# Modulation rows from unsplit weights in four column groups, and attention outputs taken by pairs of tiles, in a fused diffusion step

## The reference

```python
mod = silu(cond) @ w_ada + b_ada            # cond: 2 rows (latent, context), w_ada 1024 x 6144
shift_a, scale_a, gate_a, shift_f, scale_f, gate_f = split(mod, 6)
h = rmsnorm(x) * (1 + scale_a) + shift_a
q, k, v, g, za_f, za_b, u = split(h @ w_in)
o = gla(q, k, v, decay(za)) ; o = rmsnorm(o) * silu(g)     # 4 heads, both directions, chunks of 64
p = (pooled(u) - u) @ w_pool * pool_scale                  # 4 channel groups
x = x + gate_a * (concat(o, p) @ w_out)
h = rmsnorm(x) * (1 + scale_f) + shift_f
x = x + gate_f * expert_choice_moe(h)                      # 16 SwiGLU experts, 80 tokens each, d_ff 2816
```

## Time and profile before

| | us |
|---|---|
| median of three runs (lowest, highest) | 1903.52 (1901.79, 1906.20) |
| the profiled execution, its own time | 1903.08 |
| span of its profile | 1901.3 |
| PE busy (share of the span) | 1847.0 (97%) |
| DVE busy | 1551.7 (82%) |
| ACT busy | 1250.7 (66%) |

### The profile page before, as it was taken

How to read it: one execution, slowest core, us unless ns; L and a number is a source line. 1 busy time by engine, 2 the same in 40 slices (tenths; PEclk the granted TensorE clock), 3 DMA queues, 4 the chain that set the end, 5 groups by cost and what they waited for, 6 DMA issues and landing times.

```text
span 1901.3 us, 25073 instructions
## 1 busy us (share of the span) xinstructions
PE 1847.0 (97%) x9056; PEld 1500.9 (79%) x9056; DVE 1551.7 (82%) x1254; ACT 1250.7 (66%) x1002; POOL 272.7 (14%) x120
## 2 busy tenths in 40 slices
PE   6998879999999999999999999999999999999998
PEld 2777667668888888888888888888888888888886
DVE  4632854689889898989898989898989898989897
ACT  4433642356767676767676767676767677777774
POOL 1000000010202030303030302030303030303060
PEclk9999989989999999999999999999999999999999
DMA  8522532689999999999999999999999999999993
GB/s 287 178 76 85 184 128 89 221 313 390 389 384 390 384 381 385 368 385 373 386 372 387 372 386 371 383 373 387 375 382 374 385 372 387 372 383 370 393 378 123
DMA packets 280812, 622.83 MB, mean 328 GB/s; under 512 B 12461, under 2 KB 46018, under 8 KB 280778
## 3 DMA queue, kind: packets, MB, share of 16 engines
q1 hardware_dynamic: 273664, 598.68, 85.8%
q0 software_dynamic: 6064, 20.72, 3.7%
q10 hardware_dynamic: 1050, 2.97, 0.4%
HBM read 607.19 MB, written 15.14 MB: 327 GB/s over the span
## 4 chain that ended last, share of the span: by engine, by line
PE 93%; DVE 4%; ACT 1%; issue 1%; DMA 0%; ACTq 0%; DVEq 0%
PE bank L1831 17%; PE bank L1832 17%; PE bank L1835 17%; PE bank L1861 8%; PE bank L1857 8%; PE bank L1856 8%; PE bank L1416 3%; PE bank L1418 3%; PE bank L1417 3%; PE bank L1841 1%; PE bank L1451 1%; PE bank L1661 1%; DVE w_lo L945 1%; PE bank L1468 0%; PE bank L1469 0%
## 5 line engine op out<-in xcount | busy, mean ns | idle before, releaser
L1278 DVE TENSOR_TENSOR w_lo<-raw,w_hi 128x2048 fp32r<-128x2048 f32 x528 | 1197.7, 2288 | 121.7 <-ACT w_hi L845 119.6
L845 ACT CAST w_hi<-raw 128x2048 fp32r<-128x2048 f32 x524 | 997.8, 1913 | 181.2 <-PE bank L1835 104.3
L1831 PE MATMUL bank<-w_hi,xe_hi 128*128 128x512 f32 (+1 forms) x1536 | 573.8, 380 | 0.0
L1832 PE MATMUL bank<-w_hi,xe_lo 128*128 128x512 f32 (+1 forms) x1536 | 563.4, 373 | 0.0
L1835 PE MATMUL bank<-w_lo,xe_hi 128*128 128x512 f32 (+1 forms) x1536 | 380.4, 373 | 0.0
L1831 PEld LDWEIGHTS bank<-w_hi,xe_hi 128*128 128x128 f32 x1536 | 290.0, 189 | 49.6 <-issue 1.7
L1832 PEld LDWEIGHTS bank<-w_hi,xe_lo 128*128 128x128 f32 x1536 | 290.3, 189 | 48.5
L1835 PEld LDWEIGHTS bank<-w_lo,xe_hi 128*128 128x128 f32 x1536 | 273.4, 188 | 51.8
L1857 PE MATMUL bank<-w_hi,hT_lo 128*128 128x512 f32 x700 | 273.0, 390 | 0.0
L1856 PE MATMUL bank<-w_hi,hT_hi 128*128 128x512 f32 x700 | 272.7, 390 | 0.0
L597 POOL DMA_INDIRECT acc_dram<-yrow,idx_s x15 | 43.6, 2910 | 1072.6 <-DVE yrow L1320 1072.6
(11 more groups left out here) (264 smaller groups left out, 1367.6 us busy)
## 6 DMA issues: line engine op xcount, KB each, us to landing
raw<-in_w_e_gate SPq DMA_DIRECT2D x176, 1024.0 KB, 11.0
raw<-in_w_e_up SPq DMA_DIRECT2D x176, 1024.0 KB, 11.3
raw<-in_w_e_down SPq DMA_DIRECT2D x176, 1024.0 KB, 10.9
raw<-in_w_ada SPq DMA_DIRECT2D x16, 1024.0 KB, 5.1
raw<-in_w_in SPq DMA_DIRECT2D x8, 1024.0 KB, 5.6
ada_f<-in_w_ada SPq DMA_DIRECT2D x4, 1024.0 KB, 16.6
raw<-in_w_out SPq DMA_DIRECT2D x4, 1024.0 KB, 5.0
ada_raw<-in_w_ada SPq DMA_DIRECT2D x4, 1024.0 KB, 12.2
```

Of the source, the lines that this page charges most:

```text
L845: nc.scalar.copy(hi_slot(j), raw[:, raw_slot(j), :]).then_inc(hi_done, 1)
L1278: nc.vector.tensor_tensor(lo_slot(j), raw[:, raw_slot(j), :], hi_slot(j), ALU.subtract).then_inc(lo_done, 1)
L1831: nc.tensor.matmul(out, xe_hi[:, kk, :], wh[:, k, :], start=kk == 0, stop=False)
L1832: nc.tensor.matmul(out, xe_lo[:, kk, :], wh[:, k, :], start=False, stop=False)
```

## The change

All modulation blocks take the weights as loaded: `spread` multiplies the four blocks of contracted rows of a unit with the 32-column `cond`, each into its own 32 partitions of the bank, and the second unit (kh = 1) adds onto the first; the four partial sums are added after the turn, by a reduction in `mod_columns`. `ada_turn` turns 128 rows in place of 2 or 4, `mod_rows` copies 128. The casts and rests of the 16 ada units go; their raw slots are released by PE (`ada_used`), and the split slots are counted for the input and output projections alone (`split_count`). The position rows go to four banks without a wait between. Block 9 moves into the last tile of the loop, ahead of the pooling. `gate_a` is spread by DMA, over `gate_dram`, on POOL's queue. The pooled `mix` blocks come ahead of the attention outputs, these are taken as tiles (0, 1), (2, 3) and (4), each with its own squares and norm, and the pooled half of the first output product (tile 0, half 0) goes ahead of the turn of the heads. `gate_rows` runs in column groups too, and all of it before the choice of tokens ends.

```diff
+POS_BANKS = (4, 6, 2, 3)
+WIN_UNITS = 7
+NSPLIT = WIN_UNITS + 4
...
+def split_count(n):
+    return n - WIN0 if n < ADA0 else WIN_UNITS + n - WOUT0 + 1
 def pre_split(n):
-    return n % SPLIT if n < NPRE - 1 else SPLIT
+    if n < ADA0:
+        return (split_count(n) - 1) % SPLIT
+    return n - WOUT0
+def slot_user(n):
+    users = [q for q in range(n) if PRE[q][0] != "ada" and pre_split(q) == pre_split(n)]
+    return users[-1] if users else None
...
-        cond = keep("cond", [P, KD, P], F32R)
+        cond = keep("cond", [P, KD, 32])
+        parts_of = keep("parts_of", [P, 2])
...
+        POOL_MIX, POOL_CTX = ((4, 5), (6, 2), (7, 7), (5, 1)), 4
+        HEAD_MIX, HEAD_CTX = ((0, 5), (1, 3), (2, 4), (3, 7)), 2
...
-                        sp.wait_ge(lo_done, last[-1] + 1)
+                    if last and PRE[last[-1]][0] == "ada":
+                        _, b, kh = PRE[last[-1]]
+                        sp.wait_ge(ada_used, ada_count(b, kh))
+                    elif last:
+                        sp.wait_ge(lo_done, split_count(last[-1]))
...
+            pool.wait_ge(mod_done, ADA_FIRST + 3)
+            for st in range(2):
+                pool.dma_start(gate_dram[st].rearrange("(k p) -> p k", p=P), modT[:, 16:24, st], allow_slow_non_contiguous=True).then_inc(gate_out, 16)
+            pool.wait_ge(gate_out, 32)
+            pool.wait_ge(g_s1, TILES)
+            for st in range(2):
+                pool.dma_start(gate_a[:, st, :], gate_dram[st:st + 1, :].broadcast_to([P, D])).then_inc(gate_in, 16)
...
-                high(ADA0 + 3 + 2 * t)
-                high(ADA0 + 4 + 2 * t)
+                if t == TILES - 1:
+                    mod_rows(9)
+                    high(WOUT0)
...
+            mix_high(POOL_MIX, POOL_CTX, 0)
+            o_squares((0, 1))
             high(WOUT0 + 1)
-            mod_rows(9)
...
+            o_squares((2, 3))
+            o_squares((4,))
+            mix_high(HEAD_MIX, HEAD_CTX, HEADS + 1)
...
-                q = turn_bank(b)[:, 0:16].rearrange("p (j r) -> p j r", j=4)
+                q = turn_bank(b)[:, :].rearrange("p (q j r) -> p q r j", q=4, j=4)[:, :, 0:2, :]
                 bias = vecT[:, V_BADA + 4 * b:V_BADA + 4 * b + 4].unsqueeze(2).broadcast_to([P, 4, 2])
-                if at_ < 2:
-                    nc.vector.tensor_tensor(modT[:, 4 * b:4 * b + 4, :], q[:, :, 0:2], bias, ALU.add).then_inc(mod_done, 1)
-                    return
-                step(nc.vector.tensor_tensor(modP[:, :, :], q[:, :, 0:2], bias, ALU.add))
-                nc.vector.tensor_tensor(modT[:, 4 * b:4 * b + 4, :], modP[:, :, :], q[:, :, 2:4], ALU.add).then_inc(mod_done, 1)
+                step(nc.vector.reduce_sum(modP[:, :, 0:2], q, AX_X))
+                nc.vector.tensor_tensor(modT[:, 4 * b:4 * b + 4, :], modP[:, :, 0:2], bias, ALU.add).then_inc(mod_done, 1)
...
-                low(ADA0 + 3 + 2 * t)
-                low(ADA0 + 4 + 2 * t)
             mod_columns(ADA_FIRST + TILES - 1)
+            mod_columns(9)
+            low(WOUT0)
...
+            mix_low(POOL_MIX, POOL_CTX, 0)
+            o_norm((0, 1), 0)
             low(WOUT0 + 1)
             low(WOUT0 + 2)
-            mod_columns(9)
...
+            def spread(out, w, kh):
+                for k in range(4):
+                    last = nc.tensor.matmul(out[32 * k:32 * k + 32, :], cond[:, 4 * kh + k, :], w[:, k, :], start=kh == 0, stop=kh == 1)
+                return last
...
+                if kh == 0:
+                    if b >= ADA_FIRST:
+                        pe.wait_ge(mod_done, b)
+                    elif p >= 2:
+                        pe.wait_ge(mod_row, p - 1)
+                    elif p == 1:
+                        pe.wait_ge(x_row, 2)
+                if p < 2:
+                    pe.wait_ge(ada_in[2 * p + kh], 16)
+                    w = ada_f[2 * p + kh]
                 else:
-                    pe.wait_ge(mod_done, b)
-                for kh in range(2):
-                    split_ready(u0 + kh)
-                    wh, wl = parts(u0 + kh, 4)
-                    for k in range(4):
-                        x = cond[:, 4 * kh + k, :]
-                        nc.tensor.matmul(out, x, wh[:, k, :], start=kh + k == 0, stop=False)
-                        last = nc.tensor.matmul(out, x, wl[:, k, :], start=False, stop=kh + k == 4)
-                    last.then_inc(unit_used, 1)
+                    n = ada_unit(b) + kh
+                    pe.wait_ge(raw_full[pre_slot(n)], 16 * (pre_loads(pre_slot(n), n) + 1))
+                    w = raw[:, pre_slot(n), :]
+                spread(ada_bank(b), w.rearrange("p (k n) -> p k n", k=4), kh).then_inc(ada_used, 1)
             def ada_turn(b):
...
                 pe.wait_ge(mod_row, p + 1)
                 if 1 <= p < ADA_FIRST:
                     pe.wait_ge(mod_done, p)
-                m = 2 if p < 2 else 4
...
                 pos_rows(t)
-            pe.wait_ge(cond_hi, 1)
-            ada_unsplit(0, 0)
+            pe.wait_ge(cond_set, 1)
+            ada(0, 0)
+            ada(0, 1)
             turn_tile(0)
+            ada(2, 0)
             turn_tile(1)
-            ada_unsplit(0, 1)
-            turn_tile(2)
-            ada_unsplit(2, 0)
             pe.wait_ge(vecT_sb, 1)
             ada_turn(0)
+            ada(2, 1)
+            turn_tile(2)
             turn_tile(3)
-            ada_unsplit(2, 1)
+            ada_turn(2)
             turn_tile(4)
-            ada_turn(2)
             def decay_rows(kk):
...
             pe.wait_ge(w0_l, 1)
             first_block(0, *w0)
...
-            ada(1)
+            ada(1, 0)
+            ada(1, 1)
+            ada(3, 0)
+            ada(3, 1)
             first_block(2, *w0)
             ada_turn(1)
-            ada(3)
             first_block(3, *w0)
             ada_turn(3)
...
-                ada(ADA_FIRST + t)
+                for kh in range(2):
+                    ada(ADA_FIRST + t, kh)
                 gla_3(t)
+                if t == TILES - 1:
+                    for kh in range(2):
+                        ada(9, kh)
                 ada_turn(ADA_FIRST + t)
...
+            ada_turn(9)
             pe.wait_ge(p_sb, TILES)
-            ada(9)
-            pe.wait_ge(scan_done, HP)
-            pe.wait_ge(mod_done, ADA_FIRST + TILES + 1)
-            for t in range(TILES):
+            pe.wait_ge(mod_done, ADA_FIRST + TILES + 2)
+            for m, b in POOL_MIX:
+                nc.tensor.matmul(bank[b][:, :], wpool[:, m - HEADS, :], pT[:, m - HEADS, 0:L_LAT], start=True, stop=True).then_inc(m_ps, 1)
...
-            def same_rows(out, chunk, s, m):
-                return nc.tensor.matmul(out, modT[:, chunk, s:s + 1].broadcast_to([P, m]), ident, start=True, stop=True)
-            for q in range(4):
-                if q == 1:
-                    pe.wait_ge(mod_done, 11)
-                if q >= 2:
-                    pe.wait_ge(gate_sb, q - 1)
-                for j in range(4):
-                    last = same_rows(bank[5 + q % 2][:, j * P:(j + 1) * P], 16 + 4 * (q % 2) + j, q // 2, P)
-                last.then_inc(gate_ps, 1)
-            pe.wait_ge(gate_sb, 4)
...
+            pe.wait_ge(scan_done, HP)
+            o_rows(0)
+            o_rows(1)
+            pe.wait_ge(m_lo, 2 * HEADS)
+            o_rows(2)
+            o_rows(3)
+            o_rows(4)
...
+            pe.wait_ge(o_n, 2)
+            pe.wait_ge(m_hi, 2 * HEADS)
+            mixed(0, 0, 1, every)
+            pe.wait_ge(o_n, T_LAT)
+            for m, b in HEAD_MIX:
+                if b == 7:
+                    pe.wait_ge(o_n, TILES)
+                for t in range(T_LAT):
+                    last = nc.tensor.transpose(bank[b][:, t * P:(t + 1) * P], on[:, t, m, :], ident)
+                last.then_inc(m_ps, 1)
+            for m, _ in HEAD_MIX:
+                last = nc.tensor.transpose(bank[HEAD_CTX][:, m * P:(m + 1) * P], on[:, T_LAT, m, :], ident)
+            last.then_inc(m_ps, 1)
+            pe.wait_ge(m_hi, 4 * HEADS)
+            pe.wait_ge(m_lo, 4 * HEADS)
...
-            gate_rows(0, 0, every)
-            gate_rows(0, 1, range(2))
+            gate_rows(0, 0)
+            gate_rows(0, 1)
             turn_row(T_LAT)
-            gate_rows(0, 1, range(2, 4))
+            gate_rows(1, 0)
             logits(T_LAT)
-            gate_rows(1, 0, range(2))
+            gate_rows(1, 1)
             pe.wait_ge(r_pr, TILES)
             nc.tensor.transpose(bank[7][0:EXPERTS, P:2 * P], pr[:, T_LAT, :], ident).then_inc(r_prT, 1)
-            gate_rows(1, 0, range(2, 4))
             pe.wait_ge(topk, 1)
             nc.tensor.transpose(bank[1][0:SLOTS, EXPERTS:2 * EXPERTS], gif[:, :], ident[0:EXPERTS, 0:EXPERTS]).then_inc(idx_ps, 1)
             nc.tensor.transpose(bank[0][0:SLOTS, 0:EXPERTS], gv[:, :], ident[0:EXPERTS, 0:EXPERTS]).then_inc(idx_ps, 1)
-            gate_rows(1, 1, every)
...
```

(34 more changed lines are left out.)

279 lines of the change are left out of this document (118 added, 161 removed).

## The result

| | before | after |
|---|---|---|
| median (lowest, highest), us | 1902.95 (1901.79, 1906.20) | 1888.78 (1888.11, 1889.10) |
| ratio, 95% interval | | 0.9921 [0.9907, 0.9934] |
| span of the profile | 1901.3 | 1885.5 |

The change is faster by 14.2 us, well over what a measurement can tell, but the forecast was 38: 1865 us, range 1856 to 1884. The median lies 4.8 us above the range.

A forecast was written before the change was run, and what follows sets the result against it. TensorE was taken as the bound, the experts' loop a fixed block of 1508 us, so only its start moves: 9.5 + 3.4 + 15.9 + 9.1 + 0.5 = 38.4 us off 1903.1, 1865 us; range 1856 to 1884.

The forecast's parts named there:

- the block in four groups: Modulation blocks: four column groups run all at once, 2.0 us a block; chance 0.70.
- rival 2: Modulation blocks: column-group products run one at a time, 7.1 us a block, 1913 us, slower; chance 0.05.
- Rival 1: Modulation blocks: column groups run only two abreast, 3.7 us a block, 1881 us; chance 0.17.
- start and projections: Up to the loop: first projection product 9.5 us earlier, at 36.6 us; first projection 3.4 us shorter.
- three rounds: Scan loop: PE binds, each full round takes 7.0 us.
- 5.1 us after use, needed again after 6 to 7 us: just hidden: Scan loop: SP's weight loads through three slots land in time, so PE does not wait for them.
- `gate_a`'s load at 0 to 2 us: Scan loop: the 1 MB load of `gate_a` among SP's loads costs 0 to 2 us.
- rival 3: POOL's queue: slow element-wise store delays `x2`'s read-back, first residual waits 20 us, 1885 us; chance 0.04.
- plus 2.5 us at the low clock after a wait of 5 us: Attention outputs: 20.1 us of outputs run on, with only 2.5 us added by the low clock.
- from the output projection to the experts: Last stretch ahead of the experts: 3.2 us gain, from 2.7 us of output projection done in advance and `gate_rows`' 0.5.
- the loop's gain: Scan loop up to the first pooling product: 15.9 us gained, pooling at 224.3 us in place of 240.17.
- from the pooling to the outputs: Scans no longer hidden: outputs start 15.4 us after the pooling started, in place of 12.1.

The follow-up runs named there:

- the groups undone: Kernel with store behind scans and scans first, but each modulation unit's four products write one column group in blocks ahead of the experts: 1905.16 us, ratio 1.0011.
- Experiments 1 and 2: On the changed kernel: 1, store and broadcast moved behind the scans, 1878.82 us; 2, store left out 1882.54, in 64-byte pieces 1882.63, made twice 1893.89 us.
- both edits: Changed kernel with gate store and broadcast behind the scans, and backward scans ahead of the last modulation columns on DVE: 1859.27 us, ratio 0.9771.
- Experiments 3 and 4: On the changed kernel: 3, backward scans ahead of the last modulation columns on DVE, 1867.37 us; 4, five needless products filling TensorE's wait for the scans, 1874.01 us.
- experiment 5: Kernel before the change, with one extra VectorE operation over all of attn ahead of the last scan: median 1920.41 us, ratio 1.0067.
- experiment 4: Changed kernel with five extra 128x512 f32 products, results overwritten, while TensorE waits for the scans: 1874.01 us, ratio 0.9841.

## Why the prediction was wrong

**Right: the block in four groups.** The sum took 2.0 us between ends of 2.0 and 7.1 us; it is 1.92 with the entry, and 7.05 one at a time. Both ends were well placed, and so was rival 2's point: with the groups undone the kernel is no faster than before. Rival 1 (3.7 us a block) falls with the same row. The Trainium skill (TensorE: Matmul & The Clock Gate, Measured speedup vs the span model) has 2.38 times for three groups, from which the prediction estimated 2.4 us a block; four groups gave 3.7 times here, and the measurement decides.

**Right: start and projections.** First product at 36.46 against 36.6, the gain up to the loop 14.2 us against 12.9; three rounds of 6.97 against 7.0.

**Wrong: "5.1 us after use, needed again after 6 to 7 us: just hidden".** This term of the loop, with `gate_a`'s load at 0 to 2 us, came to 8.7 us. The landing time of 5.1 us belongs to a kernel whose loop moved 158 GB/s; the change doubles the traffic there and puts the store in it, and the median became 8.0 us. The doubled traffic alone did not break the term: with both edits the median is still 6.8 us, and the rounds stay free of waits up to the last unit. The prediction did look at the store, bounded it by 20 us, and asked only who waits for it on POOL's queue. That was rival 3, and it falls: DVE's first residual waited for PE and not for POOL's loads:

```profile
286.25 0.69 DVE L1232 TENSOR_TENSOR wtmp<-bank,gate_a 128x512 f32<-128x512 f32 x1 [2.30 <-PE bank L1450]
```

It did not ask whose transfers wait behind the store on the DMA engines. Experiments 1 and 2: 6.2 us for the 2048 pieces and, by difference, 3.8 for the broadcast, which was priced at 0 to 2.

**Wrong, and the largest: "plus 2.5 us at the low clock after a wait of 5 us".** The wait itself was foreseen (4.07 us). No row stands beside the 2.5 us; the term supposes that TensorE gets its clock back soon after the outputs start. They never got it back: 35.6 us in place of 22.6, 13 us. Experiments 3 and 4 give it back in two ways, and experiment 5 produces it in the old kernel.

**Wrong by little: from the output projection to the experts**, 1.3 in place of 3.2 us. After the 3.0 us in which TensorE stands idle ahead of 281 us, the first records of the resumed projection run at 0.63 us in place of 0.39 for some 3 us, 1.5 us lost; in the kernel before the same stretch began at full clock.

With both causes removed the loop's gain is 15.9 us, the term to the tenth. The tenth is luck, the term is not: the forecast let block 9 wait for its last unit until 209.1 us in the new clock (222 less the 12.9 gained earlier), and it waits until 207.62. The kernel then lies 5.7 us below the forecast of 1865, above all because the scans are hidden too: 12.0 us from the pooling to the outputs, where the forecast had 15.4, and no 2.5 us for the clock. So the range failed on two costs whose places were each named and priced too low: loads in the loop, and the low clock behind the wait.

## What to carry to other kernels

Here a store of 8 KB was priced by its pieces, not its bytes, and charged to whoever loaded at that time: put stores in 4-byte pieces where the DMA engines idle, or make the pieces wide. Before a long stage that may not get its clock back, as these outputs, ask what TensorE does in the last microseconds ahead of it: a short wait there can be paid for over the whole stage, so the work on the other engines that this stage waits for goes first, and if a gap can't be closed, even products for nothing in it can pay (experiment 4). When a change shortens a stage, go through the tasks that the old length had hidden, in their new order, on every queue.
